# The first norm of a two-group decoder step: sample rows normed on GpSimd, turned behind two prompt tiles, and two tiles' statistics one slice later

## The chip, the cores and the metric
One NeuronCore of a Trainium2 chip runs the whole program. The metric is the device time of one execution in microseconds (us). TensorE multiplies, VectorE and ScalarE read its accumulators, GpSimd works on SBUF alone, and SyncE issues most transfers.

## The reference
The kernel computes one layer of a hybrid decoder for two groups that share the weights: a prompt of 512 rows and samples of 8 x 4 = 32 rows, each row 1024 wide, all in float32. The part that the change touches is the very first step, the norm of the input:

```python
def layer_norm(x, g, b):
    xf = x.astype(jnp.float32)
    mu = xf.mean(-1, keepdims=True)
    var = jnp.square(xf - mu).mean(-1, keepdims=True)
    return ((xf - mu) * lax.rsqrt(var + LN_EPS) * g + b).astype(x.dtype)

hp = layer_norm(x_prompt, ln_in_g, ln_in_b)
hs = layer_norm(x_sample, ln_in_g, ln_in_b)
z = h @ w_in            # 1024 -> 2816, for hp and hs alike
```

After it come three kinds of heads (block-sparse attention, stick-breaking attention and gated mixing), an output projection, a norm, a squared-ReLU MLP of 4096 and a last norm.

## The kernel before, in words
Rows lie in five tiles: the sample tile `QT` = 4 of 32 rows and prompt tiles 0 to 3 of 128 rows. `X_ORDER` is the order of their statistics: samples first, then 0, 1, 2, 3. Step `o` counts in this order, so step 0 is the samples, step 3 is prompt tile 2 and step 4 prompt tile 3.

The first norm has two parts. In the first, each tile is normed in place with its rows on the partitions. VectorE takes statistics of 512 columns at a time (`x_stats(o, j)`, L1298), and with the second half aggregates them (L1302). ScalarE takes the root (`x_std_step`, L865). VectorE makes the factor `x_rs` (L1288) and the shift `x_sh` (L1290) in `x_scale`. ScalarE applies them to `xin` (`x_normal`, L873), in halves of 512 columns for steps 0 to 2 and whole for 3 and 4. `x_norm` counts these applications.

In the second part, the normed tiles are turned by TensorE (`turn_x`, L1918), 128 columns at a time, so that the columns lie on the partitions. A slice `q` is one column block `k = q % 8` of one half of the rows. The slices 0 to 7 hold samples and prompt tiles 0 and 1 (288 rows), the slices 8 to 15 prompt tiles 2 and 3 (256 rows). Four PSUM banks take the slices in turn. When the last tile of a slice is turned, `xt_ready` goes up. Then the gain and bias of `ln_in` are applied (`x_value` on VectorE, L1309, or for every third slice `x_own` on ScalarE, L881), giving `x_n`. ScalarE rounds it to the high part `h_hi` (`x_high`, L891), and VectorE writes the rest into `h_lo` (`x_rest`, L1320). Each product of the input projection is three matmuls, `h_hi`*`w_hi`, `h_lo`*`w_hi`, `h_hi`*`w_lo` (L1939).

TensorE begins with 4 filler matmuls on zeros, 512 columns wide (`spin`, L1912). Then it turns the first four slices of the samples, of tile 0 and of tile 1, with 2, 2 and 4 fillers of 256 columns behind them. One filler or matmul on plain float32 leaves two records in the trace. Then, for slice `q` = 0 to 7, it waits for `x_lo`, multiplies slice `q` for weight unit 0, and turns slice `q + 4` (`turn_next`). From `q` = 4 on it also multiplies for unit 1. `turn_next(4)` waits until the second half of the columns is normed in tiles 0, 1 and the samples, `turn_next(8)` until tiles 2 and 3 are normed.

Orders are written out by hand on each engine. VectorE runs statistics of steps 0 to 3, then `x_value(0)`, `x_value(1)` and a loop of `x_rest(q)` and `x_value(q + 2)`, with statistics and scales of steps 3 and 4 put between the first of them. ScalarE's loop has `x_own(q + 1)`, `x_high(q)` and the roots and norms of steps 3 and 4; at `q` = 7 and 11 it also rounds the weight units 2 and 3. GpSimd sets constants to zero, then casts weight unit 0 (L754) and subtracts (L758) as soon as its load has landed, then unit 1.

SyncE issues the loads: samples, tiles 0 and 1 in halves, constants, tile 2, weight unit 0, tile 3, weight unit 1.

Of the kernel before, what the change touches and what calls it, by code (L numbers as in the profile page):

```python
# [27 lines left out]
ALU = mybir.AluOpType  # L28
# [7 lines left out]
D_MODEL = 1024  # L36
KT = D_MODEL // P
SEQ = 512
NB = 8
NQ = 4  # L40
NS = NB * NQ
T = SEQ + NS
QT = SEQ // P
# [68 lines left out]
def hybrid_layer(nc, x_prompt, x_sample, weights, cache_k_a, cache_v_a, cache_k_b, cache_v_b,  # L112
# [14 lines left out]
    with ExitStack() as ctx:  # L127
        def sb(name, shape, dt=F32, to=None):
            return (to or ctx).enter_context(nc.sbuf_tensor(name, shape, dt))

        def sem(name):
            return ctx.enter_context(nc.semaphore(name))
# [35 lines left out]
        xin = sb("xin", [P, QT + 1, D_MODEL], to=ph)  # L168
# [5 lines left out]
        x_rs = sb("x_rs", [P, QT + 1], to=ph)  # L174
        x_sh = sb("x_sh", [P, QT + 1], to=ph)
# [107 lines left out]
        def ident(r):  # L283
            return c_("ident", r, 0, r)
# [8 lines left out]
        x_stat = sem("x_stat")  # L293
        x_std = sem("x_std")
        x_factors = sem("x_factors")
        x_norm = sem("x_norm")
        xt_ready = sem("xt_ready")

        xn_dve, xn_act = sem("xn_dve"), sem("xn_act")
# [94 lines left out]
        def x_step(q):  # L394

            hf, k = 1 - q // KT, q % KT
            bank = (s_bank[0], s_bank[1], t_bank, o_bank)[q % 4]
            return hf, k, bank[:, 0:WIDE[hf]], q % 3 == 2
# [341 lines left out]
        def _(pool):  # L740
# [9 lines left out]
            pool.memset(eps1[:, :], EPS / ALPHA ** 2).then_inc(eps1_set, 1)  # L750
            for y in range(2):
                pool.memset(qbd[y][:, :, :, :], 0.0).then_inc(zeroed, 1)
            pool.wait_ge(w_loaded[0], 16)
            pool.tensor_copy(w_hi[:, 0, :], w_raw[:, 0, :]).then_inc(w0_hi, 1)  # L754
            pool.wait_ge(w0_hi, 1)
# [75 lines left out]
            for k in range(KT):  # L831
                cols = slice(P * k, P * (k + 1))
                pool.tensor_tensor(w_raw[:, 0, cols], ln2[:, 0, cols], c_("ident"), ALU.mult).then_inc(diag_ready, 1)

            for n in range(6):
                o, j = n // 2, (1, 0)[n % 2]
                r, cols = rows[Y_ORDER[o]], slice(512 * j, 512 * (j + 1))
# [9 lines left out]
        def _(act):  # L847
            def hi_part(slot, stage, u, used, loaded):
                if used is not None:
                    act.wait_ge(half_done, used)  # L850
                act.wait_ge(w_loaded[stage], loaded)
                act.activation(w_hi[:, slot, :], w_raw[:, stage, :], ACT.Copy).then_inc(hi_done, 1)  # L852
# [7 lines left out]
            def x_std_step(o):  # L860

                t = X_ORDER[o]
                r = rows[t]
                act.wait_ge(x_stat, 3 * (o + 1))
                act.activation(x_sd[0:r, t:t + 1], x_mv[0:r, t, 1:2], ACT.Sqrt,  # L865
                               bias=eps[0:r, 0:1]).then_inc(x_std, 1)

            def x_normal(o, cols):

                t = X_ORDER[o]  # L870
                r = rows[t]
                act.wait_ge(x_factors, 2 * (o + 1))
                act.activation(xin[0:r, t, cols], xin[0:r, t, cols], ACT.Identity, bias=x_sh[0:r, t:t + 1],  # L873
                               scale=x_rs[0:r, t:t + 1]).then_inc(x_norm, 1)

            def x_own(q):

                hf, k, bank, own = x_step(q)
                if own:
                    act.wait_ge(xt_ready, q + 1)  # L880
                    act.activation(x_n[:, k, halves(hf)], bank, ACT.Identity, bias=lnp[:, 1, k:k + 1],  # L881
                                   scale=lnp[:, 0, k:k + 1]).then_inc(xn_act, 1)

            def x_high(q):

                hf, k, bank, own = x_step(q)
                if own:
                    act.wait_ge(xn_act, q // 3 + 1)
                else:
                    act.wait_ge(xn_dve, q - (q + 1) // 3 + 1)  # L890
                act.activation(h_hi[:, k, halves(hf)], x_n[:, k, halves(hf)], ACT.Copy).then_inc(x_hi, 1)  # L891

            for o in range(3):
                x_std_step(o)
                x_normal(o, slice(0, D_MODEL // 2))
            for o in range(2):
                x_normal(o, slice(D_MODEL // 2, D_MODEL))
            act.wait_ge(const_loaded, 32)
            for q in range(2 * KT):
                if q + 1 < 2 * KT:  # L900
                    x_own(q + 1)
                x_high(q)
                if q == 0:
                    x_normal(2, slice(D_MODEL // 2, D_MODEL))
                    x_std_step(3)
                if q == 1:
                    x_normal(3, slice(0, D_MODEL))
                if q == 2:
                    x_std_step(4)
                if q == 4:  # L910
                    x_normal(4, slice(0, D_MODEL))
                if q == 7:
                    hi_part(2, 0, 2, None, 32)
                if q == 11:
                    hi_part(3, 1, 3, None, 32)
# [356 lines left out]
            for j in range(2):  # L1272
                act.wait_ge(y_gained, j + 1)
                cols = slice(512 * j, 512 * (j + 1))
# [7 lines left out]
        def _(dve):  # L1282
            def x_scale(o):

                t = X_ORDER[o]
                r = rows[t]
                dve.wait_ge(x_std, o + 1)
                dve.reciprocal(x_rs[0:r, t:t + 1], x_sd[0:r, t:t + 1]).then_inc(x_factors, 1)  # L1288
                dve.wait_ge(x_factors, 2 * o + 1)
                dve.scalar_tensor_tensor(x_sh[0:r, t:t + 1], x_mv[0:r, t, 0:1], -1.0, x_rs[0:r, t:t + 1],  # L1290
                                         ALU.mult, ALU.mult).then_inc(x_factors, 1)

            def x_stats(o, j):

                t = X_ORDER[o]
                r = rows[t]
                dve.wait_ge(x_half_loaded[t] if t < 2 and j == 0 else x_loaded[t], 16)
                dve.bn_stats(x_st[0:r, t, 6 * j:6 * j + 6],  # L1298
                             xin[0:r, t, 512 * j:512 * (j + 1)]).then_inc(x_stat, 1)
                if j:  # L1300
                    dve.wait_ge(x_stat, 3 * o + 2)
                    dve.bn_aggr(x_mv[0:r, t, :], x_st[0:r, t, :]).then_inc(x_stat, 1)  # L1302

            def x_value(q):

                hf, k, bank, other = x_step(q)
                if not other:
                    dve.wait_ge(xt_ready, q + 1)
                    dve.tensor_scalar(x_n[:, k, halves(hf)], bank, lnp[:, 0, k:k + 1], lnp[:, 1, k:k + 1],  # L1309
                                      ALU.mult, ALU.add).then_inc(xn_dve, 1)  # L1310

            def x_rest(q):

                hf, k, bank, other = x_step(q)
                dve.wait_ge(x_hi, q + 1)
                if other:
                    dve.wait_ge(xn_act, q // 3 + 1)
                else:
                    dve.wait_ge(xn_dve, q - (q + 1) // 3 + 1)
                dve.tensor_tensor(h_lo[:, k, halves(hf)], x_n[:, k, halves(hf)],  # L1320
                                  h_hi[:, k, halves(hf)].bitcast(F32), ALU.subtract).then_inc(x_lo, 1)
# [8 lines left out]
            x_stats(2, 1)  # L1330
            x_scale(2)
            x_stats(3, 0)
            x_stats(3, 1)
            dve.wait_ge(const_loaded, 32)
            x_value(0)
            x_value(1)
            for q in range(2 * KT):
                x_rest(q)
                if q == 0:
                    x_scale(3)  # L1340
                if q + 2 < 2 * KT:
                    x_value(q + 2)
                if q in (0, 1):
                    x_stats(4, q)
                if q == 3:
                    x_scale(4)

            def read_half(u):
# [558 lines left out]
        def _(pe):  # L1907
            def spin(count, width=SEQ):

                zeros = qbd[0][:, :, :, :].rearrange("p b c q -> p (b c q)")  # L1910
                for _ in range(count):
                    pe.matmul(acc[:, 0, 0:width], zeros[:, 0:P], zeros[:, 0:width], start=True, stop=True)  # L1912

            def turn_x(q, t):

                hf, k, bank, _ = x_step(q)
                at = 0 if t == QT else NS + P * t if t < 2 else P * (t - 2)
                mm = pe.transpose(bank[:, at:at + rows[t]], xin[0:rows[t], t, P * k:P * (k + 1)], ident(rows[t]))  # L1918
                if t in (1, 3):
                    mm.then_inc(xt_ready, 1)  # L1920

            pe.wait_ge(zeroed, 2)
            spin(4)
            pe.wait_ge(const_loaded, 32)
            for o, t in enumerate((QT, 0, 1)):
                pe.wait_ge(x_norm, o + 1)
                for q in range(4):
                    turn_x(q, t)
                spin((2, 2, 4)[o], SEQ // 2)

            def product(wh, wl, slot, cols, hi, lo, ks, out, hf, part=slice(None), fresh=True):

# [31 lines left out]
            def turn_next(q):  # L1964

                if q == 4:
                    pe.wait_ge(x_norm, 6)
                if q == KT:
                    pe.wait_ge(x_norm, 8)
                for t in (QT, 0, 1) if q < KT else (2, 3):  # L1970
                    turn_x(q, t)

            for q in range(KT):
# [629 lines left out]
```

## Time and profile before

| | |
|---|---|
| median of 3 runs | 682.44 us (681.54 to 683.45) |
| profiled execution | 685.94 us |
| its span | 684.20 us |
| TensorE matmul busy | 668.9 us, 98% of the span |
| VectorE / ScalarE / GpSimd busy | 424.2 / 321.5 / 408.0 us |
| mean granted clock of TensorE | 0.988 |

The profiled execution has 1.74 us around its span and is 3.50 us above the median. Times in the rows count from the start of the span. A timeline row gives start, duration, engine, line and operation, what it writes and reads, and the number of instructions merged into the row; in brackets stands the idle time before it and what ended it. A row of several instructions runs from the start of the first to the end of the last. Matmuls are pipelined, so starts are more reliable than ends.

### The profile page before, as it was taken

Reading aid. Unit: us, or ns where it says so; the run is one execution under the profiler, and the core shown is the slowest. Engines: PE = TensorE matmul, PEld = TensorE weight load, DVE = VectorE, ACT = ScalarE, POOL = GpSimd, SP = SyncE. Lnnn points to the kernel's source line nnn. Section 1 sums busy time; section 2 is a strip of 40 time slices with the busy share of each in tenths; the row PEclk is TensorE's granted clock in tenths of the full one; section 3 lists DMA queues with packets and bytes.
Section 4 is the critical chain, followed back from the end, with each engine's and each line's share of the span. In section 5 each row is a group of like instructions: output and inputs, shape, how many; then the busy total and the mean of one; then the engine's idle time right before and its main releaser. Section 6 shows DMA issues by size and latency. Waiting matters only on the chain.

```text
span 684.2 us, 14030 instructions
## 1 busy us (share of the span) xinstructions
PE 668.9 (98%) x5499; PEld 642.0 (94%) x5499; DVE 424.2 (62%) x798; ACT 321.5 (47%) x640; POOL 408.0 (60%) x502
## 2 busy tenths in 40 slices
PE   7999999999999899999999999999999999999996
PEld 4999999999998569999999999999999999999995
DVE  7647555576653735578987584774856747636246
ACT  6666656677755514555453533334425234253122
POOL 4554433333443405422898996968959869688417
PEclk9899999999999989999999999999999999999999
DMA  6343321313429843110531321522313115124003
GB/s 229 118 155 126 94 75 50 93 62 93 140 62 343 273 147 124 62 63 1 186 103 55 134 81 62 165 83 70 116 62 125 62 63 185 62 93 155 1 1 131
DMA packets 34006, 73.66 MB, mean 108 GB/s; under 512 B 3988, under 2 KB 19380, under 8 KB 33942
## 3 DMA queue, kind: packets, MB, share of 16 engines
q1 hardware_dynamic: 26822, 68.88, 30.0%
q10 hardware_dynamic: 6864, 3.90, 1.9%
q8 instruction: 44, 0.72, 0.4%
q14 instruction: 20, 0.16, 0.1%
q0 software_dynamic: 256, 0.00, 0.0%
HBM read 67.16 MB, written 5.60 MB: 106 GB/s over the span
## 4 chain that ended last, share of the span: by engine, by line
PE 89%; DVE 3%; DMA 2%; SPq 2%; ACT 1%; issue 1%; POOL 0%; ACTq 0%; DVEq 0%
PE acc L1939 27%; PE acc L2330 21%; PE acc L2300 7%; PE s_bank L2359 3%; PE s_bank L2358 3%; PE s_bank L2357 3%; PE o_bank L2047 2%; PE acc L2359 2%; PE acc L2358 2%; PE acc L2357 2%; PE acc L2318 1%; PE acc L2317 1%; PE acc L2319 1%; PE acc L2033 1%; PE t_bank L2033 1%
## 5 line engine op out<-in xcount | busy, mean ns | idle before, releaser
L745 POOL TENSOR_TENSOR w_lo<-w_raw,w_hi 128x256 fp32r<-128x256 f32 x144 | 121.9, 878 | 160.6 <-ACT w_hi L852 160.6
L825 POOL TENSOR_TENSOR w_lo<-w_raw,w_hi 128x256 fp32r<-128x256 f32 x142 | 119.2, 878 | 31.8 <-ACT w_hi L1226 31.8
L1939 PE MATMUL acc<-h_hi,w_hi 128*128 128x288 f32 (+1 forms) x416 | 130.2, 313 | 2.6 <-DVE h_lo L1320 2.1
L1939 PE MATMUL acc<-h_lo,w_hi 128*128 128x288 f32 (+1 forms) x416 | 120.4, 289 | 0.0
L1939 PE MATMUL acc<-h_hi,w_lo 128*128 128x288 f32 (+1 forms) x416 | 120.3, 289 | 0.0
L1939 PEld LDWEIGHTS acc<-h_hi,w_hi 128*128 128x128 f32 x416 | 79.2, 190 | 5.6 <-DVE h_lo L1320 3.0
L1226 ACT ACTIVATE w_hi<-w_raw 128x512 fp32r<-128x512 f32 x71 | 43.9, 629 | 84.6 <-PE acc L2330 54.5
L1939 PEld LDWEIGHTS acc<-h_lo,w_hi 128*128 128x128 f32 x416 | 79.3, 191 | 0.3
L2330 PE MATMUL acc<-m_hi,w_lo 128*128 128x256 f32 (+1 forms) x384 | 79.2, 287 | 0.0
L2330 PE MATMUL acc<-m_hi,w_hi 128*128 128x256 f32 (+1 forms) x384 | 79.1, 287 | 0.0
L2330 PE MATMUL acc<-m_lo,w_hi 128*128 128x256 f32 (+1 forms) x384 | 79.1, 287 | 0.0
L1939 PEld LDWEIGHTS acc<-h_hi,w_lo 128*128 128x128 f32 x416 | 78.8, 190 | 0.0
L1877 DVE TENSOR_TENSOR res<-res,acc 128x256 f32<-128x256 f32 x96 | 37.6, 432 | 54.7 <-PE acc L2330 54.7
L2330 PEld LDWEIGHTS acc<-m_lo,w_hi 128*128 128x128 f32 x384 | 61.7, 188 | 0.0
L2330 PEld LDWEIGHTS acc<-m_hi,w_lo 128*128 128x128 f32 x384 | 61.5, 188 | 0.0
L2330 PEld LDWEIGHTS acc<-m_hi,w_hi 128*128 128x128 f32 x384 | 61.4, 188 | 0.0
L825 POOL TENSOR_TENSOR w_lo<-s_sum,w_hi 128x256 fp32r<-128x256 f32 x60 | 46.8, 812 | 16.0 <-ACT w_hi L1226 16.0
L852 ACT ACTIVATE w_hi<-w_raw 128x1024 fp32r<-128x1024 f32 x36 | 38.1, 1058 | 16.4 <-DMA w_raw<-weights 9.2
L825 POOL TENSOR_TENSOR more_lo<-w_raw,more_hi 128x256 fp32r<-128x256 f32 x42 | 36.9, 909 | 0.0
L1374 DVE TENSOR_TENSOR q_st<-z_q,q_st 64x256 fp32r<-64x256 f32 x48 | 20.6, 429 | 26.1 <-ACT q_st L951 25.0
L1226 ACT ACTIVATE w_hi<-s_sum 128x512 fp32r<-128x512 f32 x30 | 18.4, 627 | 39.2 <-PE acc L2330 31.2
L825 POOL TENSOR_TENSOR more_lo<-s_sum,more_hi 128x256 fp32r<-128x256 f32 x36 | 32.3, 927 | 3.6 <-ACT more_hi L1226 3.6
(396 smaller groups left out, 1855.2 us busy)
## 6 DMA issues: line engine op xcount, KB each, us to landing
w_raw<-weights SPq DMA_DIRECT2D x94, 512.0 KB, 3.5
k_t<-cache_k_a SPq DMA_DIRECT2D x16, 192.0 KB, 3.7
k_t<-cache_k_b SPq DMA_DIRECT2D x16, 192.0 KB, 4.1
v_pg<-cache_v_a SPq DMA_DIRECT2D x8, 192.0 KB, 4.4
v_pg<-cache_v_b SPq DMA_DIRECT2D x8, 192.0 KB, 4.2
k_t<-cache_v_b SPq DMA_DIRECT2D x8, 192.0 KB, 4.5
y_prompt<-y_n SPq DMA_DIRECT2D x6, 256.0 KB, 2.2
xin<-x_prompt SPq DMA_DIRECT2D x4, 256.0 KB, 3.8
```

Of the source, the lines that this page charges most:

```text
L745: op = pool.tensor_tensor(w_lo[:, slot, part], w_raw[:, stage, part], w_hi[:, slot, part].bitcast(F32), ALU.subtract)
L825: op = pool.tensor_tensor(lo[:, cols], src[:, cols], hi[:, cols].bitcast(F32), ALU.subtract)
L852: act.activation(w_hi[:, slot, :], w_raw[:, stage, :], ACT.Copy).then_inc(hi_done, 1)
L1226: act.activation(part_at(i)[0], src, ACT.Copy).then_inc(part_hi, 1)
L1374: dve.tensor_tensor(q_st[OWN[1 - (h ^ order)], h, order, cols], z, hi, ALU.subtract).then_inc(q_stack_lo, 1)
L1877: dve.tensor_tensor(res[:, m, halves(hf)], res[:, m, halves(hf)], acc[:, 2 * (m % 2) + hf, 0:WIDE[hf]], ALU.add).then_inc(acc_dve, 1)
L1939: mm = pe.matmul(out, w[:, slot, cols(k)], x[:, ks[k], halves(hf)], start=(fresh and k == 0 and pas == 0), stop=last)
L2300: mm = pe.matmul(acc[:, at + hf, 0:WIDE[hf]], (w_hi, w_hi, w_lo)[pas][:, slot, cols(k)], (hi, lo, hi)[pas][:, ks[k], halves(hf)], start=(k ...
L2330: mm = pe.matmul(acc[:, at + hf, 0:WIDE[hf]], (whi, whi, wlo)[pas][:, cols], (m_hi, m_lo, m_hi)[pas][:, FG * par + f, halves(hf)], start=( ...
L2357: pe.matmul(out, whi[:, w], hi, start=(k == 0), stop=False)
L2358: pe.matmul(out, whi[:, w], lo, start=False, stop=False)
L2359: mm = pe.matmul(out, wlo[:, w], hi, start=False, stop=(k == KT // 2 - 1))
```

## The change
The samples' two applications of factor and shift go from ScalarE to GpSimd, where they stand between the memsets and the first weight cast and count a semaphore of their own, `xs_norm`. TensorE turns tiles 0 and 1 before the samples, in the first four slices and in `turn_next`; `xt_ready` of the slices 0 to 7 is now raised by the samples' turn. The fillers behind the three tiles are 4, 2 and 2 instead of 2, 2 and 4. On VectorE the second half of the statistics of step 3 goes from before `x_value(0)` to behind `x_rest(0)`, and everything of steps 3 and 4 behind it goes one slice later. On ScalarE the root and norm of steps 3 and 4 go one slice later too.

```diff
-        x_norm = sem("x_norm")
+        x_norm, xs_norm = sem("x_norm"), sem("xs_norm")
...
+            pool.wait_ge(x_factors, 2)
+            for cols in (slice(0, D_MODEL // 2), slice(D_MODEL // 2, D_MODEL)):
+                pool.tensor_scalar(xin[0:NS, QT, cols], xin[0:NS, QT, cols], x_rs[0:NS, QT:QT + 1], x_sh[0:NS, QT:QT + 1],
+                                   ALU.mult, ALU.add).then_inc(xs_norm, 1)
             pool.wait_ge(w_loaded[0], 16)
...
             for o in range(3):
                 x_std_step(o)
-                x_normal(o, slice(0, D_MODEL // 2))
-            for o in range(2):
-                x_normal(o, slice(D_MODEL // 2, D_MODEL))
+                if o:
+                    x_normal(o, slice(0, D_MODEL // 2))
+            x_normal(1, slice(D_MODEL // 2, D_MODEL))
...
                 if q == 0:
                     x_normal(2, slice(D_MODEL // 2, D_MODEL))
+                if q == 1:
                     x_std_step(3)
-                if q == 1:
+                if q == 2:
                     x_normal(3, slice(0, D_MODEL))
-                if q == 2:
+                if q == 3:
                     x_std_step(4)
-                if q == 4:
+                if q == 5:
                     x_normal(4, slice(0, D_MODEL))
...
             x_stats(3, 0)
-            x_stats(3, 1)
             dve.wait_ge(const_loaded, 32)
             x_value(0)
             x_value(1)
             for q in range(2 * KT):
                 x_rest(q)
                 if q == 0:
+                    x_stats(3, 1)
+                if q == 1:
                     x_scale(3)
                 if q + 2 < 2 * KT:
                     x_value(q + 2)
-                if q in (0, 1):
-                    x_stats(4, q)
-                if q == 3:
+                if q in (1, 2):
+                    x_stats(4, q - 1)
+                if q == 4:
                     x_scale(4)
...
-                if t in (1, 3):
+                if t == (QT if hf else 3):
                     mm.then_inc(xt_ready, 1)
...
-            for o, t in enumerate((QT, 0, 1)):
-                pe.wait_ge(x_norm, o + 1)
+            for o, t in enumerate((0, 1, QT)):
+                pe.wait_ge(*((xs_norm, 1) if t == QT else (x_norm, o + 1)))
                 for q in range(4):
                     turn_x(q, t)
-                spin((2, 2, 4)[o], SEQ // 2)
+                spin((4, 2, 2)[o], SEQ // 2)
...
                 if q == 4:
+                    pe.wait_ge(x_norm, 4)
+                    pe.wait_ge(xs_norm, 2)
+                if q == KT:
                     pe.wait_ge(x_norm, 6)
-                if q == KT:
-                    pe.wait_ge(x_norm, 8)
-                for t in (QT, 0, 1) if q < KT else (2, 3):
+                for t in (0, 1, QT) if q < KT else (2, 3):
                     turn_x(q, t)
```

## Rows read from the trace of the kernel before

**Rows 1.** TensorE's waits: engine, line, releaser, us in total, times, longest.
```profile
PE t_bank L2084 <- DMA k_t<-cache_k_b: 2.3, 1, 2.3
PE acc L1939 <- DVE h_lo L1320: 2.1, 3, 1.0
```

**Rows 2.** Timeline of 7 to 13 us: start, duration, instruction, idle before.
```profile
7.14 0.16 DVE L1290 SCALAR_TENSOR_TENSOR x_sh<-x_mv,x_rs 128x1 f32<-128x1 f32 x1
...
7.34 0.81 ACT L873 ACTIVATE xin<-xin,x_sh,x_rs 128x512 f32<-128x512 f32 x1 [0.52 <-DVE x_sh L1290]
...
7.38 0.31 PE L1918 MATMUL s_bank<-cst,xin 32*128 32x32 f32 x2
...
7.74 1.13 PE L1912 MATMUL acc<-qbd 128*128 128x256 f32 x4
...
8.71 0.38 PE L1918 MATMUL s_bank<-cst,xin 128*128 128x128 f32 x2
...
8.91 2.22 ACT L873 ACTIVATE xin<-xin,x_sh,x_rs 128x512 f32<-128x512 f32 x3 [0.43 <-DVE x_sh L1290]
...
9.14 1.03 PE L1912 MATMUL acc<-qbd 128*128 128x256 f32 x4
...
9.84 1.28 DVE L1298 BATCH_NORM_STATS2 x_st<-xin 128x6 f32<-128x512 f32 x2 [0.97 <-DMA xin<-x_prompt]
10.01 0.38 PE L1918 MATMUL s_bank<-cst,xin 128*128 128x128 f32 x2
...
11.14 1.04 POOL L754 CAST w_hi<-w_raw 128x1024 fp32r<-128x1024 f32 x1 [8.91 <-DMA w_raw<-weights]
...
11.29 1.03 DVE L1309 TENSOR_SCALAR x_n<-s_bank,lnp 128x288 f32<-128x288 f32 x2
...
12.40 0.89 DVE L1320 TENSOR_TENSOR h_lo<-x_n,h_hi 128x288 fp32r<-128x288 f32 x1
```

**Rows 3.** Groups by line and form, GpSimd: count | busy us, mean ns.
```profile
L842 POOL TENSOR_TENSOR y_n<-y_n,ln 32x512 f32<-32x512 f32 x2 | 2.8, 1420 | 0.2
```

**Rows 4.** Timeline of 13 to 21 us, the loop over the slices.
```profile
13.49 0.42 DVE L1290 SCALAR_TENSOR_TENSOR x_sh<-x_mv,x_rs 128x1 f32<-128x1 f32 x1
...
14.43 0.46 DVE L1320 TENSOR_TENSOR h_lo<-x_n,h_hi 128x288 fp32r<-128x288 f32 x1
...
16.26 0.29 ACT L865 ACTIVATE x_sd<-x_mv,eps 128x1 f32<-128x1 f32 x1 [0.72 <-DVE x_mv L1302]
...
16.79 0.57 ACT L881 ACTIVATE x_n<-s_bank,lnp 128x288 f32<-128x288 f32 x1
...
16.84 0.61 PE L1939 MATMUL acc<-h_hi,w_hi 128*128 128x288 f32 x1 [0.68 <-DVE h_lo L1320]
...
17.30 0.44 ACT L891 ACTIVATE h_hi<-x_n 128x288 fp32r<-128x288 f32 x1
...
18.32 1.24 ACT L873 ACTIVATE xin<-xin,x_sh,x_rs 128x1024 f32<-128x1024 f32 x1 [0.57 <-DVE x_sh L1290]
...
18.43 0.59 PE L1939 MATMUL acc<-h_hi,w_hi 128*128 128x288 f32 x1
...
20.88 0.63 PE L1918 MATMUL s_bank<-cst,xin 128*128 128x128 f32 x2
```

**Rows 5.** Stretches: length, busy us by engine, granted clock, DMA share, GB/s.
```profile
16.84:22.95 6.11, 6.11 (x24) 5.39 (x25) 4.22 (x10) 4.22 (x9) 3.10 (x4) 0.50 0.44 161
...
23.00:33.50 10.50, 10.50 (x87) 10.43 (x86) 7.70 (x15) 7.28 (x21) 6.63 (x8) 1.00 0.29 96
...
50.00:54.00 4.00, 2.63 (x21) 2.44 (x20) 3.18 (x12) 2.61 (x8) 0.88 (x2) 1.00 1.04 372
...
238.60:244.90 6.30, 6.28 (x69) 2.55 (x73) 2.69 (x5) 1.66 (x3) 0.00 (x0) 0.50 1.02 360
```

**Rows 6.** Timeline of SyncE's queue, 195 to 250 us.
```profile
219.60 0.34 SPq L663 DMA_DIRECT2D wsp<-w_spatial  x1
...
227.09 2.14 SPq L605 DMA_DIRECT2D k_t<-cache_k_b  x4
```

## The prediction, made before the changed kernel ran

> **What bounds the kernel now.** I read the page's engine shares, then TensorE's waits over the whole span, then the timeline of the first 30 us. TensorE is busy 98% of the span (the table above), and its longest waits are few: 2.3 us once for a cache transfer, and 2.1 us in three pieces for `h_lo`, VectorE's part of the first norm [rows 1]. The edit touches only the first norm, so it can move the time by what it does to TensorE before some 33 us and by what later stages make of the shift. Elapsed time in this stage goes to three things. First, VectorE waits for prompt tile 2 and then spends 1.28 us on its statistics before it scales the first column slice at 11.29 [rows 2]. Second, VectorE, ScalarE and VectorE again make each slice in a chain, and TensorE waits for it until 16.84 [rows 1, 4]. Third, the granted clock is 0.50 (1.2 GHz) from 16.84 to 22.95 [rows 5]; there TensorE is busy all the time, and two turns take 0.63 us against 0.38 at full clock [rows 2, 4].
>
> **Part 1: the sample rows go to GpSimd.** GpSimd does nothing between its memsets and its cast at 11.14 [rows 2]; the samples' factors are ready before those of tile 0 at 7.30 (7.14 + 0.16). A scale-and-shift of 32x512 on GpSimd is in no row. The nearest are the 128x1024 cast, 1.04 us, so 0.52 for half the columns, and the two-input 32x512 operation of L842, 1.42 us [rows 2, 3]. Two of them end by 8.3 to 10.1 us, before the cast and before their first reader. I take the cast's price, as it too has one input; the result is the same at either end. Cost 0, hidden in idle GpSimd; without that cover it would be 1 to 2.8 us ahead of the weight cast. ScalarE loses two operations of at most 0.81 us each, but its first prompt normal starts when `x_sh` is there (7.30, then 7.34), and its second at 8.91 for the same reason [rows 2]. So what ScalarE saves is idle time: gain 0, and not below zero by itself. What can be lost is VectorE's time: `x_sh` of a prompt tile took 0.16 us at 7.14 with GpSimd idle and 0.42 at 13.49 with GpSimd busy [rows 2, 4], so up to +0.3 for tile 0.
> The Trainium skill (GPSIMD Engine Reference, Key points) says that GpSimd shares its SBUF interfaces with VectorE, and that they collide when a VectorE instruction has two SBUF inputs. The two durations just named agree; by the rule, if the second GpSimd half is still running at 7.14, the whole start is 0.3 later.
>
> **Part 2: TensorE's order.** This is the term that decides. Before, the samples are turned at 7.38, ahead of everything, and the first slice is complete when tile 1 is turned, at 10.01. Filler matmuls stand between the turns, 2, 2 and 4 of them; two take 0.87 us (9.14 to 10.01), one 0.43 [rows 2]. They are in TensorE's queue, so a turn behind them waits. After the edit:
> Tile 0 is normed at 7.34 + 0.81 = 8.15. Tile 1 went from 9.72 (8.91 + 0.81) to its turn at 10.01, 0.30 later, so tile 0 is turned at 8.45. Its turns take 0.43 (8.71 to 9.14), the four fillers behind them 1.73, and from a filler's end to the next turn it is 0.1 (7.74 + 0.87 = 8.61, turn at 8.71). Tile 1, normed at 9.72, therefore waits for fillers and is turned at 10.7.
> From one turn over two fillers to the next is 1.30 (8.71 to 10.01): the samples are turned at 12.0, with their first result 0.3 later (two of their turns took 0.31 at 7.38). `xt_ready` now counts these turns, so VectorE's first scaling starts at about 12.3.
>
> **Part 3: half a tile's statistics behind the first slice.** Half the statistics is 0.64 and the aggregate 0.17 (9.84 + 1.28 = 11.12, scaling at 11.29) [rows 2], together 0.8 from before the first scaling; by itself VectorE could begin at 9.84 + 0.64 = 10.5 instead of 11.29, a gain of 0.8. But it now idles until 12.3. The gain is covered by the new wait, and the sum for the first slice is 12.3 - 11.29 = +1.0.
> The same 0.8 us comes back inside the loop, and one half of tile 3's statistics (0.64) and the aggregate go out past `h_lo` 2. From the first scaling to TensorE's third slice was 16.84 - 11.29 = 5.55 us [rows 2, 4]; the VectorE work in between is the same to 0.2 us, so the third slice starts at about 17.85. Queued behind the statistics are `x_rest(1)` on VectorE and with it TensorE's second slice; nothing there is hidden, as TensorE waits anyway.
>
> **Part 4: the steps one slice later.** Nothing is issued or removed in number; what counts is tile 3, since `turn_next(8)` waits for `x_norm` 6 (was 8, the same operation). Before, tile 3 was normed at 18.32 + 1.24 = 19.56, and the turns stood at 20.88, so there was 1.3 us of slack [rows 4]. After, from the end of `h_lo` 2 at 17.8: scaling 0.5 (half of 1.03), second half of the statistics and aggregate 0.8 (19.1), ScalarE's root 0.3 (19.4), its own scaling of slice 5 and the high part of slice 4, 0.51 + 0.44 (20.35), VectorE's rest 0.46 (20.8), shift 0.42 and about 0.15 for the reciprocal ahead of it (21.4), norm 1.24 (22.65), 0.30 to the turn: 22.95. The durations are those of [rows 2, 4]. That is +2.1 against 20.88.
> TensorE itself would be there sooner. At the low clock a slice takes 18.43 - 16.84 = 1.59 us [rows 4]; from 17.85 that gives 19.45, 19.75 (waiting for `h_lo` 3), 21.35, and under half a slice for the three matmuls ahead of the turns: 22.05. So it would stand still for about 0.9 us, a wait for ScalarE that the trace of before does not have. At full clock the stall is longer and the end the same.
> Behind it I see full work: in 23 to 33.5 us TensorE was busy 10.50 of 10.50 us, VectorE and ScalarE only 7.70 and 7.28 [rows 5]. So no slack gives the 2.1 us back.
>
> **The clock's term.** Before, it was low for 22.95 - 20.88 = 2.07 us of the work behind this turn; low time costs half of itself. If it has risen by the time of the new turn, 1.0 comes back: +1.1. If it stays low as long again, +2.1. If it stays low for another 6.1 us, as after the idle time that ended at 16.84, +4.1. Rows speak for the longer: both rises of the trace follow 6.1 us (16.84 to 22.95) and 6.3 us (238.6 to 244.9) without a stall [rows 5]. A stall of 0.9 us falls into this stretch now. The middle of 0 and 6.1 is 3.1 and gives 2.1 + (3.1 - 2.07)/2 = +2.6. I take 0.2 off, as the 0.89 us of the first `h_lo` [rows 2] against 0.46 of the next [rows 4] may not recur: **+2.4**.
> The Trainium skill (TensorE: Matmul & The Clock Gate, A second HAM failure mode) describes small idle times between groups of matmuls that make the clock alternate between its two levels. By that rule the low stretch would be the longer one, up to +4.1; the trace agrees in so far as its clock fell amid waits of 1.0, 0.4 and 0.7 us (2.1 in three [rows 1]; 0.68 the last [rows 4]).
>
> **Later stages.** The next stage starts with reads of the accumulators that TensorE fills here, and the cache transfers for the 2.3 us wait are issued only when VectorE's `m_lo`, which follows TensorE, has let SyncE's queue go on, from 219.60 [rows 6]. So they shift with TensorE, and I count 0 for them.
>
> **Sum.** The profiled execution took 685.94 us: 684.20 of span and 1.74 around it. It is 3.50 above the median 682.44. 685.94 + 2.4 = 688.3; less 3.50, that is 684.8 in the scale of the median. A measurement of this kernel can tell about 0.3% (2.05 us) from no change, so this lies just past that bound.
>
> **Rivals.**
> A, the forecast: the new wait for tile 3 and a low clock behind it, +1.9 to +4.1, so 684.3 to 686.5. Chance 0.46.
> B: the same late turns, but the clock is up by then. +1.1; with the whole chain 0.7 us quicker (uncontended `h_lo` operations and the filler row's edges) +0.4, with 0.3 of contention and a partly low clock +1.9. So 682.8 to 684.3. For it: at 50 to 54 us TensorE was busy 2.63 of 4.00 us and kept its full clock [rows 5]. Chance 0.34.
> C: no difference, because the operations take less than in this trace, or a later wait absorbs the shift. The place would be the 2.3 us wait before 238.6. Against it: the transfers before that wait are issued from 227.09 on, behind 219.60 in the queue [rows 6], and so shift too. -0.4 to +0.4. Chance 0.10.
> D, faster: the shift changes TensorE's 2.3 us stall that ends at 238.6 so that the clock does not fall there. Up to half of the 6.3 us at 1.2 GHz, 3.1, would be saved: 1.1 - 3.1 = -2.0, or 680.4. It decides from the point where that stall is under about 1 us. Against it: the DMA engines are full there (share 1.02 in [rows 5]), so transfers would bound that stage instead. Chance 0.04.
> E: the clock falls already in the prologue, since TensorE has nothing to do from about 7.4 to 8.4 once the sample turns are gone from there. Fillers would take twice as long: 6 x 0.43 = +2.6 more, +5 in all, 687.4. Against it again 50 to 54 us. Chance 0.06.
> **How the numbers follow.** A's part below +2.05 is about 0.03 of its chance. Slower by over 0.3%: 0.43 + 0.06 = 0.49, less 0.01 for rounding in A: 0.48. Faster by over 0.3%: 0.04, and 0.01 for what I do not see: 0.05. Within: the rest, 0.47. The range leaves out D, E and most of C: 682.7 to 686.4.
>
> **What the profile after would show.** The first filler group behind tile 0 has 8 records and tile 1's turn stands at 10.6 to 10.8, not 10.0; the 32-column turns come at about 12.0; VectorE idles from 10.5 to about 12.3; the first `h_lo` matmul stands at 14.0 to 14.4; tile 3's norm ends at 22.3 to 22.8 and TensorE has a wait for `xin` of 0.5 to 1.2 us in front of the turns. The clock row rises after 23. It would be wrong if the first scaling stands at 10.5 to 11.3 (fillers shorter than I read them), if tile 3's norm is early, or if the clock never falls.

## The result, and the profile after

| | before | after |
|---|---|---|
| median | 683.45 us (7 runs, 681.54 to 685.60) | 687.80 us (7 runs, 684.82 to 688.79) |
| ratio to before | | 1.0063, 95% interval 1.0044 to 1.0082 |
| profiled execution | 685.94 us | 684.82 us |
| its span | 684.20 us | 683.00 us |
| mean granted clock in it | 0.988 | 0.989 |

The changed kernel is 4.35 us (0.6%) slower. The forecast was slower too, by 2.4 us, but its range ended at 686.4, 4.0 above the median it started from, and the measured median lies above it. There is a trap in the table: the two profiled executions stand the other way round, and the one of after is the fastest of its seven. So the traces are read stage by stage, not by their totals.

The prologue after, all engines: start, duration, instruction, idle before. It answers to [rows 2].

```profile
5.61 1.52 POOL L755 TENSOR_SCALAR xin<-xin,x_rs,x_sh 32x512 f32<-32x512 f32 x2 [3.38 <-DVE x_sh L1295]
...
7.00 0.16 DVE L1295 SCALAR_TENSOR_TENSOR x_sh<-x_mv,x_rs 128x1 f32<-128x1 f32 x1
...
8.15 0.41 PE L1924 MATMUL s_bank<-cst,xin 128*128 128x128 f32 x2 [0.79 <-ACT xin L877]
...
8.61 1.89 PE L1918 MATMUL acc<-qbd 128*128 128x256 f32 x8
...
10.34 0.38 PE L1924 MATMUL s_bank<-cst,xin 128*128 128x128 f32 x2
...
10.59 0.69 DVE L1303 BATCH_NORM_STATS2 x_st<-xin 128x6 f32<-128x512 f32 x1 [1.87 <-DMA xin<-x_prompt]
...
11.74 0.31 PE L1924 MATMUL s_bank<-cst,xin 32*128 32x32 f32 x2
...
12.10 1.06 DVE L1314 TENSOR_SCALAR x_n<-s_bank,lnp 128x288 f32<-128x288 f32 x2 [0.82 <-PE t_bank L1924]
```

TensorE turns tile 0 at 8.15, runs eight filler records, turns tile 1 at 10.34 and the samples at 11.74. VectorE has its statistics at 11.28 and then waits 0.82 us for those turns. The first scaling stands at 12.10, against 11.29 in [rows 2].

The loop after, same columns, with the read of the first accumulator that ends the stage. It answers to [rows 4].

```profile
17.77 0.61 PE L1945 MATMUL acc<-h_hi,w_hi 128*128 128x288 f32 x1 [0.52 <-DVE h_lo L1325]
...
21.76 1.24 ACT L877 ACTIVATE xin<-xin,x_sh,x_rs 128x1024 f32<-128x1024 f32 x1 [1.23 <-DVE x_sh L1295]
...
23.05 0.69 PE L1924 MATMUL s_bank<-cst,xin 128*128 128x128 f32 x2 [0.81 <-ACT xin L877]
...
36.23 0.39 ACT L942 ACTIVATE z_q<-acc 128x256 f32<-128x256 f32 x1 [1.06 <-PE acc L1945]
```

Tile 3's norm ends at 23.00, TensorE stands still for 0.81 us and turns slice 8 at 23.05. It waited for nothing there before, at 20.88 [rows 4]. The same read of the accumulator stood at 33.59 before:

```profile
33.59 0.39 ACT L937 ACTIVATE z_q<-acc 128x256 f32<-128x256 f32 x1 [1.08 <-PE acc L1939]
```

So the stage is 2.64 us longer. The shift is the same at 209 us: the sample scores start at 209.21 before and at 211.86 after, 2.65 later. The clock's part shows in two stretches, first after, then before: length, TensorE's busy time, granted clock, DMA share, GB/s.

```profile
16.25:23.00 6.75, 5.47 (x20) 0.50 0.45 124
23.00:26.25 3.25, 3.20 (x14) 0.50 0.18 69
```

```profile
16.25:23.00 6.75, 6.17 (x25) 0.50 0.45 155
23.00:26.25 3.25, 3.25 (x27) 1.00 0.02 5
```

After, the clock is at 1.2 GHz until 26.25, before until 23.01, so it rises 3.2 us later. In the same 3.25 us, busy nearly throughout both times, TensorE has 14 matmul records instead of 27.

Then 3.5 us come back: the last sample values start at 251.04, before at 251.87. In between TensorE waits for a transfer of cache keys. These are the wait after the change (us, times, longest), and the stretch around it (length, busy time of TensorE's matmuls, its weight loads, VectorE, ScalarE and GpSimd, granted clock, DMA share, GB/s):

```profile
PE t_bank L2091 <- DMA k_t<-cache_k_b: 0.5, 1, 0.5
```

```profile
235.00:250.00 15.00, 14.40 (x185) 10.56 (x180) 8.57 (x17) 2.71 (x8) 0.00 (x0) 1.00 0.91 322
```

The wait is 0.5 us, where [rows 1] has 2.3, and the clock stays at 1.00 from 235 to 250 us, where before it was 0.50 for 6.8 us, most of them in [rows 5]. TensorE comes to this wait 3.70 us later than before (240.00 against 236.30), but the keys let it go on only 1.91 us later (240.53 against 238.62); so the wait shrinks. This may be why the execution is the fastest of its kernel. It is not shown, as the other six have no trace, and their mean clocks, 0.986 to 0.990, don't all lie below this one's 0.989.

### The profile page after: what moved, and what is told of

It reads as the page before. It is cut to its first block, busy times and chain, and to the rows that moved or that the text cites. A ratio compares the mean times of both kernels' runs of the same rounds, so it can differ in the third digit from the quotient of the medians.

```text
span 683.0 us, 14031 instructions
## 1 busy us (share of the span) xinstructions
PE 667.9 (98%) x5499; PEld 642.0 (94%) x5499; DVE 424.4 (62%) x798; ACT 319.6 (47%) x638; POOL 409.7 (60%) x504
## 4 chain that ended last, share of the span: by engine, by line
PE 89%; DVE 4%; ACT 2%; DMA 2%; SPq 2%; issue 1%; POOL 0%; ACTq 0%; DVEq 0%
PE acc L1945 26%; PE acc L2337 21%; PE acc L2307 7%; PE s_bank L2366 3%; PE s_bank L2365 3%; PE s_bank L2364 3%; PE o_bank L2054 2%; PE acc L2366 2%; PE acc L2365 2%; PE acc L2364 2%; PE acc L2325 1%; PE acc L2324 1%; PE acc L2326 1%; PE acc L2040 1%; PE t_bank L2040 1%
## 5 line engine op out<-in xcount | busy, mean ns | idle before, releaser
L829 POOL TENSOR_TENSOR more_lo<-s_sum,more_hi 128x256 fp32r<-128x256 f32 x36 | 32.3, 926 | 3.6 <-ACT more_hi L1231 3.6
```

Source lines behind the costliest of these rows:

```text
L829: op = pool.tensor_tensor(lo[:, cols], src[:, cols], hi[:, cols].bitcast(F32), ALU.subtract)
```

## The experiments

Each kernel ran with the kernel before on the same chip; before's median is 682.8 to 683.3 us there. A mean granted clock is given for every run; over the 29 runs of before on one of these chips, the ten with 0.995 or more have a median of 682.2 us and the ten with 0.991 or less 684.0. So within one kernel the executions with a lower clock are 1.8 us slower; how much of that is the clock and how much the waits that come with it, these means don't tell.

**late_before** and **late_after**: the stretch at 236 us, filled in both kernels.

```diff
+                if gi == 3:
+                    pe.wait_ge(s_probs_written, gi)
+                    for _ in range(16):
+                        pe.matmul(s_score_bank(gi)[:, 0:SK], id_r[:, :], sb_r[:, gi, :], start=True, stop=True)
                 for n in range(4 * gi, 4 * gi + 4):
                     pe.wait_ge(*keys_sem(n))
```

> The kernel before, with 16 filler matmuls of 288 columns (about 0.12 us each, 1.9 us in all) on TensorE ahead of its wait for the cache keys of the fourth sample group, near 236 to 238 us; their result is overwritten. Theory 1 (in some executions of either kernel the clock falls in this wait and costs some 3 us; the rest of the difference is the start): the clock stays at 1.00 between 235 and 250 us in the profile, and the median falls from about 683.4 to about 682, with a smaller spread. Rival (this stretch plays no part): the median stays within 0.5 us of the kernel before.

> The changed kernel with the same 16 fillers in the same place. Theory 1: the median falls from 687.8 to about 684.8, so that it stands 2.7 us above late_before, which is the shift of 2.65 us that the two profiles show from 33 to 222 us. Rival (the executions outside the profile lose the further 1.7 us at the start, by a longer low clock there): the median stays at 686.5 or more, over 4 us above late_before.

Measured: late_before 681.93 us, ratio 0.9984 (0.9968 to 0.9999), 1.3 below before. late_after 687.05, ratio 1.0058 (1.0036 to 1.0080), against 1.0063 (1.0044 to 1.0082) without fillers: no difference clear of noise. The clock is at 1.00 from 235 to 250 us in both profiles. But late_after did not fall to 684.8, and the gap is 5.1 us, not 2.7. Theory 1 falls: most of the loss is at the start, as its rival has it. The late stretch is worth about 1 us to before and nothing clear of noise to the changed kernel, and the profiles show a reason. This is the wait for the keys, first after, then late_after with the fillers (L2082) in it:

```profile
239.15 0.84 PE L2224 MATMUL s_bank<-s_cst,s_own 128*128 128x16 f32 x6
240.53 0.37 PE L2091 MATMUL t_bank<-sb_r,id_r 128*128 128x288 f32 x1 [0.53 <-DMA k_t<-cache_k_b]
```

```profile
240.54 2.35 PE L2082 MATMUL t_bank<-sb_r,id_r 128*128 128x288 f32 x16
```

In late_after the work ahead of the fillers starts at 239.85 and the first matmul behind them at 242.73, 2.88 us later, where after has 1.38. The last keys had landed at 241.54. So here the fillers outlast the wait that they fill. They are equally long in both kernels, so they don't change the gap between the two.

The two profiles show how much the start varies:

```profile
31.96 0.39 ACT L937 ACTIVATE z_q<-acc 128x256 f32<-128x256 f32 x1 [1.08 <-PE acc L1939]
```

```profile
37.17 0.39 ACT L942 ACTIVATE z_q<-acc 128x256 f32<-128x256 f32 x1 [1.05 <-PE acc L1945]
```

late_before reads the accumulator at 31.96 with the clock at 1.00 up to there, late_after at 37.17 with 10.2 us of low clock. These are 5.2 us, with the same first-stage code as in the pair above that differs by 2.64. The low stretch of late_after is as long as that of after, so what makes its start 0.9 us later is not a longer one, as the rival had it; its waits for `h_lo` are longer, 3.1 us against 1.9.

**order_only**: the changed kernel with VectorE's and ScalarE's loops as before. **loop_only**: the kernel before with only these loops changed. The core of order_only against the changed kernel; loop_only has the reverse of it against before:

```diff
             x_stats(3, 0)
+            x_stats(3, 1)
             dve.wait_ge(const_loaded, 32)
...
                 if q == 0:
-                    x_stats(3, 1)
-                if q == 1:
                     x_scale(3)
...
-                if q in (1, 2):
-                    x_stats(4, q - 1)
-                if q == 4:
+                if q in (0, 1):
+                    x_stats(4, q)
+                if q == 3:
                     x_scale(4)
```

> The changed kernel with the loops of VectorE and ScalarE as before: only the samples on GpSimd, TensorE's order of turns and the fillers 4, 2, 2 stay. Theory 1 (the start's 2.65 us is 0.8 from TensorE's order and fillers and the rest from tile 3's norm coming one slice later): first scaling at 12.1, tile 3 normed at about 20.4, the turns of slice 8 at about 21.6 without a wait for xin, and the stage at 209 us shifted by 0.7 to 1.2 us against before. Rival (the order of turns costs all of it): shift 2 us or more with the turns of slice 8 at 22.5 or later.

> The kernel before with only the loops of VectorE and ScalarE changed: samples on ScalarE, order of turns and fillers 2, 2, 4 as before, the steps of tiles 2 and 3 one slice later. Theory 1: first scaling at 10.5 instead of 11.3, tile 3 normed at about 21.2, so the turns of slice 8 at about 21.5, 0.6 later than before, with a wait for xin of 0.5 us or more; shift at 209 us between 0 and +1.5 us, depending on when the clock rises. Rival (the later statistics gain their 0.8 us once the turns' order is out of the way): shift -0.8 us.

Measured: order_only 685.55 us, ratio 1.0040 (1.0022 to 1.0057); loop_only 686.07, ratio 1.0054 (1.0033 to 1.0075). Either part alone makes the kernel slower. In order_only the first scaling stands at 12.32 (expected 12.1), tile 3 is normed at 20.95 (20.4), and the turns of slice 8 come at 22.24 (21.6) and do not wait for it, as expected; the clock is low for 6.8 us and the shift at 209 us is 1.28 (expected up to 1.2). In loop_only the first scaling stands at 10.94 (expected 10.5), tile 3 is normed at 22.39 (21.2), TensorE waits 0.7 us for it, the clock is low for 10.2 us, and the shift is 2.28, outside what I expected. No sign of a gain from the later statistics. Together the two ratios stand 0.9% above 1, more than the 0.6% of the whole change, so with the clock free the parts don't add.

**tile3_early**: only the last two steps of tile 3, its factors and its norm, put back by one slice.

```diff
-                if q == 5:
+                if q == 4:
                     x_normal(4, slice(0, D_MODEL))
...
-                if q == 4:
+                if q == 3:
                     x_scale(4)
```

> The changed kernel with only the last step of tile 3 put back by one slice: its factors behind slice 3 instead of 4 on VectorE, its norm behind slice 4 instead of 5 on ScalarE. Theory 2 (the wait for tile 3 is one of two parts of the loss): tile 3 normed at about 21.5 instead of 23.0, no wait or one under 0.3 us ahead of the turns of slice 8, the accumulator read 1 to 2 us earlier than in the changed kernel, median 685.3 to 686.8. Rival (the order of the turns costs all): median within 0.5 us of 687.8.

Measured: 686.36 us, ratio 1.0053 (1.0036 to 1.0070). Tile 3 is normed at 21.61, there is no wait ahead of the turns, and the accumulator is read at 35.43, 0.8 earlier than after. The clock is low for 6.8 us here and for 10.2 after. So in the profiles this wait costs something, but it is not the whole; the ratios, 1.0053 and 1.0063, are too near to tell the two kernels apart.

**gpsimd_only**: the kernel before with only the samples' norm on GpSimd, turned first as before.

> The kernel before with only the samples' norm moved to GpSimd: turns, fillers and both loops as before. Both theories: no change, 683.2 within 0.7 us; GpSimd ends its two halves by 7.2 us and `x_sh` of tile 0 is not later than 7.3. The rival of the prediction's part 1 (a contention that delays tile 0): +0.3 us.

Measured: 683.70 us, ratio 1.0010 (0.9994 to 1.0026). GpSimd's two halves take 1.52 us together and end at 7.08; `x_sh` of tile 0 starts at 7.11 and takes 0.16. No difference, as both said.

**hold_before** and **hold_after**: TensorE's waits of the first norm filled too, so that the clock does not fall in either kernel. The late fillers stay. The edit of hold_after; hold_before has the prologue's fillers 2, 2, 6, `{0: (1, 256), 1: (1, 384)}` behind the slices and none ahead of slice 8's turns:

```diff
-                spin((4, 2, 2)[o], SEQ // 2)
+                spin((4, 2, 4)[o], SEQ // 2)
...
                 first_unit(0, q)
+                if q == 4:
+                    spin(3, SEQ // 2)
                 turn_next(q + 4)
+                spin(*{0: (1, 384), 1: (2, 320), 2: (1, 384), 3: (1, 384)}.get(q, (0, SEQ)))
```

> The kernel before with fillers also where TensorE waits in the first norm: 2 more behind the prologue's turns, one of 256 columns behind slice 0 and one of 384 behind slice 1, and the 16 fillers of late_before. Theory 2 (the two kernels differ by waits for the norms, and by how long the clock is low at the start): the clock is at 1.00 from 12 to 34 us, ScalarE reads the first accumulator at 31.9 to 32.3 us, the median is 681.0 to 682.0, at most late_before. Rival (the clock plays no part in the first stage, the spread has another source): the median stays within 0.3 us of late_before's 681.9 and the spread is as before.

> The changed kernel with fillers in its waits of the first norm (2 more behind the prologue's turns, 0.6 to 0.7 us behind the slices 0 to 3 each, three more ahead of the turns of slice 8) and the 16 late ones. Theory 2: the clock stays at 1.00, the turns of slice 8 still come at 23 us as they wait for tile 3's norm, ScalarE reads the first accumulator at 34.6 to 35.1 instead of 37.2 in late_after; the median falls from 687.05 to about 685, and stands 3.2 us above hold_before: that is the price of the waits alone. Rival (the low clock is the whole difference): the median comes to within 1 us of hold_before.

Measured: hold_before 681.49 us (680.29 to 682.09), ratio 0.9977 (0.9963 to 0.9991). hold_after 684.78 (683.91 to 685.25), ratio 1.0022 (1.0007 to 1.0038). The gap is 3.29 us, where 3.2 was expected, and the twelve runs of each kernel now lie within 1.8 us, where 35 of before's lay within 6.0. The accumulator is read at 31.48 and 35.49, outside the 31.9 to 32.3 and 34.6 to 35.1 that were expected. The waits are there with the clock at 1.00 throughout:

```profile
12.84 1.06 DVE L1314 TENSOR_SCALAR x_n<-s_bank,lnp 128x288 f32<-128x288 f32 x2 [2.78 <-PE s_bank L1924]
```

```profile
22.08 1.24 ACT L877 ACTIVATE xin<-xin,x_sh,x_rs 128x1024 f32<-128x1024 f32 x1 [0.94 <-DVE x_sh L1295]
```

```profile
23.63 0.38 PE L1924 MATMUL s_bank<-cst,xin 128*128 128x128 f32 x2
```

In hold_after VectorE had its data ready and waited 2.78 us for TensorE's turns. Some 0.7 us of that belong to this execution: the second half of tile 0 landed late (VectorE waited 0.50 us for it), and `x_sh` of tile 0 stands at 7.74, where after and late_after have 7.00 and 6.96. The turns of slice 8 come 0.31 us behind the end of tile 3's norm at 23.32. In hold_before the same three are at 10.18, 17.35 and 18.64:

```profile
10.18 1.03 DVE L1309 TENSOR_SCALAR x_n<-s_bank,lnp 128x288 f32<-128x288 f32 x2
...
17.35 1.24 ACT L873 ACTIVATE xin<-xin,x_sh,x_rs 128x1024 f32<-128x1024 f32 x1 [0.70 <-DVE x_sh L1290]
...
18.64 0.44 PE L1918 MATMUL s_bank<-cst,xin 128*128 128x128 f32 x2 [0.21 <-ACT xin L873]
```

The changed kernel loses time to the clock of the first stage: from late_after to hold_after the median falls by 2.3 us. From late_before to hold_before it falls by 0.4, which is within the noise. The late and the hold runs come from two chips, but the ratios to before give much the same, 2.5 and 0.5.

**hold_order**, **hold_loop** and **hold_fewer**: the parts one by one, with the clock held. They are order_only, loop_only and hold_after with the fillers of their expectations.

> order_only (samples on GpSimd, turned last, fillers 4, 2, then 4 behind the samples; both loops as before) with the waits of the first norm filled as in hold_before and the 16 late fillers. Theory 3 (with the clock held, the 3.3 us between hold_after and hold_before are two terms that add: 1.3 to 2.1 from the later first scaling, 1.5 to 2.0 from tile 3's later norm): first scaling at 12.1 to 12.8, everything behind it as in hold_before, accumulator read at 33.1 to 33.8, median 682.8 to 683.6, so 1.3 to 2.1 above hold_before. Rival (one wait hides the other, so that either alone costs nearly all): 3 us above hold_before.

> loop_only (both loops changed, samples and order of turns as before) with the waits filled as in hold_after and the 16 late fillers. Theory 3: first scaling at 10.0 to 11.0 as the statistics' second half is out of its way; tile 3 normed 10.5 us behind it; turns of slice 8 at 21 to 21.8 against 18.6 in hold_before; accumulator read at 32.8 to 33.6; median 1.5 to 2.1 above hold_before, 683.0 to 683.6. Rival: 3 us above.

> hold_after with the prologue's fillers 2, 0, 6 instead of 4, 2, 4: the order of the turns stays (tile 0, tile 1, samples), but no filler stands between tile 1 and the samples and two fewer behind tile 0. Theory 3 (of the turns' order only the fillers ahead of the samples cost): samples turned at 10.2 to 10.6, first scaling at 10.6 to 11.3, tile 3 normed at 21 to 21.9, median 1.5 to 2.1 above hold_before, equal to hold_loop within 0.4. Rival (to turn the samples last costs by itself): median at hold_after's 684.8.

| with the clock held | first scaling | tile 3 normed | accumulator read | median | above hold_before |
|---|---|---|---|---|---|
| hold_before | 10.18 | 18.59 | 31.48 | 681.49 | |
| hold_order | 12.27 | 20.45 | 32.80 | 682.66 | 1.17 |
| hold_loop | 10.50 | 21.56 | 33.53 | 683.04 | 1.55 |
| hold_fewer | 10.96 | 22.03 | 34.17 | 683.42 | 1.93 |
| hold_after | 12.84 | 23.32 | 35.49 | 684.78 | 3.29 |

The order of the turns with its fillers costs 1.2 us, the loops cost 1.6, together 2.7 of the 3.3. So they nearly add, which speaks for theory 3 and against one wait hiding the other; the 0.6 left over was not taken apart. hold_order's median came out 0.1 below the range expected of it and its accumulator was read 0.3 earlier; in hold_loop tile 3 was normed 11.1 us behind the first scaling (expected 10.5), in hold_fewer at 22.03 (expected up to 21.9).

hold_fewer keeps the order of the turns, but drops the fillers ahead of the samples: 1.4 of 3.3 us go away. It lies 0.4 above hold_loop, and by the ratios not above it at all, so the order itself costs little and the fillers in front of the samples' turns cost most of that term. The last three ran on another chip than hold_before and hold_after. Their ratios to before, 0.9993, 1.0004 and 1.0002 against 0.9977 and 1.0022, give 1.1, 1.8, 1.7 and 3.1 us above hold_before, with intervals of about 0.0015 to either side, 1 us: the order of size stands, 0.3 us doesn't.

hold_before beats both kernels: 0.23% faster than before (0.09% to 0.37%). It is the old schedule with fillers in four places where TensorE waits.

## Why the prediction was right or wrong

**GpSimd's part: right.** Two halves took 1.52 us, between the ends of 1.04 and 2.84, in idle GpSimd. The contention of up to 0.3 did not come: `x_sh` took 0.16 us at 7.00, although GpSimd worked until 7.13, and gpsimd_only shows no difference clear of noise. So the rule of the Trainium skill (GPSIMD Engine Reference, Key points) had next to nothing to act on here; 0.13 us of overlap neither supports nor refutes it.

**TensorE's order: right in its mechanism, short in one end.** Forecast: turns at 8.45, 10.7 and 12.0, scaling at 12.3. Profile: 8.15, 10.34, 11.74 and 12.10. The whole is 0.2 to 0.4 earlier, because tile 0 was normed 0.15 earlier and its turn followed after 0.15 us and not after 0.30. VectorE idled for 0.82 us and not from 10.5 on, since tile 2 landed later than before. But +1.0 was counted from before's 11.29, and that number belongs to one landing of tile 2, at 9.84 in [rows 2]. Its statistics started between 8.5 and 10.6 us in the profiles here. The old order starts to scale some 1.5 us behind them, at 10.18 in hold_before and 10.41 in gpsimd_only; the new one waits for the samples' turns and scales at 12.06 even where the statistics started at 9.32, as in late_after. The term is 0.8 for the tile as late as in [rows 2] and 1.9 for an early one, and I had only the first. In all six profiles with the new order and its 4 and 2 fillers, the first scaling stands 5.10 or 5.11 us behind the start of `x_sh` of tile 0, wherever tile 2 landed: the chain of turns and fillers sets it alone.

**The loops: right, in part by luck.** Third slice forecast at 17.85, found at 17.77. Tile 3 normed forecast at 22.65, found at 23.00; stall forecast 0.9, found 0.81; turns forecast at 22.95, found at 23.05. The norm was 0.35 later than forecast and the turn followed it after 0.05 us instead of 0.30, so two misses nearly cancel. That the 0.8 us of the statistics come back inside the loop held in hold_loop too: from the first scaling to the third slice it took 5.99 us there, against 5.52 in hold_before.

**The clock behind the stall: right, by a guess.** It stayed low for 3.2 us behind the turns, and the forecast had taken 3.1, the middle between 0 and 6.1, without a reason for the middle. In late_after it was low for 4.6 us behind the same turns. The two low stretches of before, which the prediction read as 6.1 and 6.3 us, lasted 6.8 us each (16.18 to 23.01 and 238.05 to 244.88); 6.1 and 6.3 were the lengths of the rows. In the pair of profiles the stage is 2.64 us longer, where +2.4 was forecast.

**The step that failed is the sum**, the sentence "It is 3.50 above the median 682.44 ... less 3.50". I carried a difference between profiles over to the medians, as if the 3.50 were common to both kernels. It is not: that execution had both low stretches and a late tile 2. late_before's profile has the same first scaling (11.31) but no low stretch, and its start is 1.63 us shorter (31.96 against 33.59). So my baseline already held a large part of the loss that the changed kernel shows in every profile. The term "2.07 us low before" was subtracted at its full size, although some of before's executions have no such stretch: late_before and gpsimd_only, whose first stage is the old one or as good as it, stay at 1.00, and the ten of 29 runs with the highest clock are 1.8 us faster than the ten with the lowest. Both profiles of the changed first stage have 10.2 us of it.

What the runs showed in its place: the accumulator is read at 33.59, 31.96 and 31.15 with the old first stage (before, late_before, gpsimd_only) and at 36.23 and 37.17 with the new one (after, late_after). The means are 4.5 us apart, and of the six pairs the one of the forecast, 2.64, is the closest. The medians differ by 4.35 us, where +2.4 was forecast. A further 1.0 us of the distance to the 684.8 of the forecast is the median of before, 682.44 from three runs and 683.45 from seven.

The 5.1 us between late_after and late_before can be divided with the hold runs into 3.3 of waits, 2.3 of clock in the changed kernel, less 0.4 of clock in before. This is a division and no test, since the parts are differences of the same medians. Of the way from 5.1 to the 4.35 measured without fillers, it is only shown that the fillers take about 1 us off before and nothing clear of noise off the changed kernel.

**The rivals.** D's mechanism came true in the profiled execution, where the stall at 236 us shrank to 0.5, the clock stayed up, and 3.5 us came back. The medians did not get faster, and whether the changed kernel's other executions have it no trace shows. The transfers did not bound that stage as I had argued. That the stall must come under about 1 us did not hold: in loop_only it was 1.5 us, and the clock stayed up too. I had counted 0 for the later stages because TensorE and the transfers would shift together; at this wait they shifted by 3.70 and 1.91 us. The wait is 0.5 in after's profile and 1.5 to 2.3 in those of before, loop_only, order_only, tile3_early and gpsimd_only; why the two shifts differ so was not settled. E, the clock falling in the prologue, did not happen: TensorE was idle for 0.8 us there in after and for 1.7 in hold_after, and the turns and fillers ran at full rate.

## What to carry to other kernels

Filler work that keeps an in-order engine busy is free only behind the last thing that someone waits for; put ahead of it, it becomes a wait of up to its own length, and so does filler that is longer than the wait it fills. A step that has slack in the profile, like tile 3's norm with its 1.3 us, can lose more than its slack when it is moved by one slice, because the chain of two engines behind it moves too: it ends 3.0 us later in hold_loop than in hold_before. And before a difference worked out on one trace is carried to medians, look how far that execution is from the median and why: a stretch that only some executions have must enter the sum at its share, not at its full size.

## What the runs showed of the hardware

Prompt tile 2, issued near 4 us each time, let its statistics start anywhere from 8.5 to 10.6 us; where VectorE waited for it, it landed between 9.3 and 10.6. The granted clock differs as well between executions of one kernel; in the first 34 us before showed 6.8 us at half rate in one profile, and late_before, with the same code there, none, with nearly the same waits for `h_lo` (2.1 and 1.9 us in three). The Trainium skill (TensorE: Matmul & The Clock Gate, What's actually happening) says of the matmuls at the low clock at a kernel's start that their number varies from run to run with one kernel. No profile here bears on the start, but for a low stretch in the middle of a kernel these two show the same kind of difference.

Around the stall at 236 us the clock stayed at 1.00 where the stall took 0.5 and 1.5 us (after, loop_only), was low for 3.4 us where it took 1.9, 2.0 and 2.1 (order_only, tile3_early, gpsimd_only) and for 6.8 us where it took 2.3 (before). These are six single executions.

Fillers of zeros in the waits of the first stage, which took 0.4 to 1.5 us without them, came with a clock of 1.00 from 12 to 34 us in all five profiles with them; of the eight without, two had it. The spread over twelve runs went from 3.5 us (late_before) to between 0.8 and 1.8; before's own 35 runs spread over 6.0.

What VectorE loses to a busy GpSimd is not a fixed 0.3 us. `x_sh` of a prompt tile took 0.16 us with GpSimd idle. In 18 places of the 13 profiles it met a cast or a subtraction on GpSimd and took 0.42 to 0.80 us, and each time it ended 0.01 to 0.03 us after that GpSimd instruction: in loop_only it ran from 14.80 to 15.60 and the cast until 15.59. So it looks as if VectorE waits for the instruction that GpSimd is in, and loses what is left of it. In one place, in hold_order, it took 0.16 us beside a subtraction that had 0.09 us left.
